# Two unused buffers shift the on-chip addresses of the split weights and of the matmuls' moving operands

## The reference

```python
for l in range(DEPTH):                       # DEPTH = 2
    hp = _modulate(xp, norm1_g[l], ...)      # RMSNorm, shift, scale
    ...                                      # l = 0: differential attention || GQA
    ...                                      # l = 1: mLSTM || latent attention
    xp = xp + mod_p[2] * out_p
    hp = _modulate(xp, norm2_g[l], ...)
    xp = xp + mod_p[5] * _conv_ffn(hp, ffn_w_up[l], ffn_conv_w[l], ffn_conv_b[l], ffn_w_down[l])
    ...                                      # the same for the latent tokens xs
```

## Time and profile before

| | |
|---|---|
| median of three executions | 2651.89 us (2647.7 to 2652.81) |
| the profiled execution | 2675.88 us, of which the span from first to last instruction is 2674.1 us |
| TensorE matmul busy | 2550.9 us, 95% of the span |
| VectorE, ScalarE busy | 1485.3 us, 1295.8 us |
| mean granted clock of TensorE | 0.976 |

### The profile page before, as it was taken

The page is one execution under the profiler, slowest core; times in us unless marked ns, Lnnn a source line. Parts: engine busy times, 40 slices in busy tenths (PEclk is TensorE's granted clock), DMA queues, the critical chain, the costliest instruction groups (busy, mean ns, idle before and its releaser), DMA issues. The chain is left out here.

```text
span 2674.1 us, 52531 instructions
## 1 busy us (share of the span) xinstructions
PE 2550.9 (95%) x20826; PEld 2328.3 (87%) x20826; DVE 1485.3 (56%) x1970; ACT 1295.8 (48%) x1795; POOL 11.7 (0%) x20
## 2 busy tenths in 40 slices
PE   6799999989999999999989999789899999999997
PEld 1487988878888888899989889778899999999997
DVE  1334455655454545577765445645655565567676
ACT  1443444364444444466565444334655555556553
POOL 0000000000000000000000000000000000000000
PEclk9999999989999999999989998889899999999999
DMA  9886665768888888865646884123455555555553
GB/s 388 330 317 233 231 228 184 289 256 309 318 316 319 314 318 313 321 212 192 203 128 234 321 299 142 62 93 114 156 189 186 184 187 185 185 188 187 176 186 107
DMA packets 170060, 608.28 MB, mean 227 GB/s; under 512 B 18688, under 2 KB 25152, under 8 KB 169648
## 3 DMA queue, kind: packets, MB, share of 16 engines
q1 hardware_dynamic: 168624, 600.33, 64.0%
q10 hardware_dynamic: 512, 2.97, 0.3%
q0 software_dynamic: 768, 2.79, 0.3%
HBM read 601.38 MB, written 4.63 MB: 227 GB/s over the span
## 5 line engine op out<-in xcount | busy, mean ns | idle before, releaser
L498 DVE TENSOR_TENSOR w_lo<-raw,w_hi 128x1024 fp32r<-128x1024 f32 x756 | 925.5, 1225 | 966.3 <-ACT w_hi L491 964.6
L491 ACT ACTIVATE w_hi<-raw 128x1024 fp32r<-128x1024 f32 x756 | 798.7, 1057 | 1018.2 <-PE banks L638 994.2
L636 PE MATMUL banks<-xs_ffn,w_hi 128*128 128x256 f32 x4224 | 1188.3, 281 | 5.2 <-DVE xs_ffn L792 5.0
L637 PE MATMUL banks<-xs_ffn,w_hi 128*128 128x256 f32 x4224 | 1181.9, 280 | 0.0
L638 PE MATMUL banks<-xs_ffn,w_lo 128*128 128x256 f32 x4224 | 1181.7, 280 | 0.0
L636 PEld LDWEIGHTS banks<-xs_ffn,w_hi 128*128 128x128 f32 x4224 | 797.8, 189 | 43.5 <-issue 42.6
L638 PEld LDWEIGHTS banks<-xs_ffn,w_lo 128*128 128x128 f32 x4224 | 803.8, 190 | 0.0
L637 PEld LDWEIGHTS banks<-xs_ffn,w_hi 128*128 128x128 f32 x4224 | 795.3, 188 | 0.0
L592 PE MATMUL banks<-raw,cond 128*32 128x512 f32 x1536 | 227.2, 609 | 29.2 <-DMA raw<-in_w_mod 18.0
L636 PE MATMUL banks<-xs_even,w_hi 128*128 128x256 f32 x832 | 241.8, 291 | 10.0 <-DVE w_lo L498 5.9
L637 PE MATMUL banks<-xs_even,w_hi 128*128 128x256 f32 x832 | 233.3, 280 | 0.0
(11 more groups left out here) (305 smaller groups left out, 2054.2 us busy)
## 6 DMA issues: line engine op xcount, KB each, us to landing
raw<-in_w_mod SPq DMA_DIRECT2D x384, 512.0 KB, 6.7
raw<-in_ffn_w_up SPq DMA_DIRECT2D x352, 512.0 KB, 3.5
raw<-in_ffn_w_down SPq DMA_DIRECT2D x176, 512.0 KB, 4.1
raw<-in_even_w_in SPq DMA_DIRECT2D x72, 512.0 KB, 4.0
raw<-in_odd_w_in SPq DMA_DIRECT2D x64, 512.0 KB, 4.5
raw<-in_even_w_out SPq DMA_DIRECT2D x32, 512.0 KB, 3.7
raw<-in_odd_w_out SPq DMA_DIRECT2D x32, 512.0 KB, 3.2
raw<-in_odd_w_tail SPq DMA_DIRECT2D x8, 448.0 KB, 3.7
```

Source lines behind the costliest of these rows:

```text
L491: act.activation(w_hi[:, o % SPLIT], raw[:, s % RAW], ACT.Copy).then_inc(hi_done.sem, 1)
L498: dve.tensor_tensor(w_lo[:, o % SPLIT], raw[:, s % RAW], w_hi[:, o % SPLIT].bitcast(F32), ALU.subtract).then_inc(lo_done.sem, 1)
L636: pe.matmul(made, hi, x_hi, start=start and not second, stop=False, skip_group_check=second)
L637: pe.matmul(made, hi, x_lo, start=False, stop=False, skip_group_check=second)
```

## The change

Two buffers that nothing reads or writes are declared: 96 columns of 4 bytes (384 bytes a partition) between `raw` and `w_hi`, and 16 columns (64 bytes) behind `m0`. By this `w_hi` and `w_lo`, `x` and `const` move by 384 bytes, and all that the stages declare by 448. After it the split weights and the moving operands of all stages begin at multiples of 512 bytes; so before it the split weights began 128 bytes, and the moving operands 64 bytes, behind such a multiple. The tiles inside these buffers step by multiples of 512 bytes. No instruction is added, removed or moved.

```diff
         raw = sb("raw", [P, RAW, CHUNKS, SLABW])
+        weight_pad = sb("weight_pad", [P, 96])
         w_hi = sb("w_hi", [P, SPLIT, CHUNKS, SLABW], F32R)
         w_lo = sb("w_lo", [P, SPLIT, CHUNKS, SLABW], F32R)
...
         m0 = sb("m0", [2 * HEADS, 2])
+        stage_pad = sb("stage_pad", [P, 16])
```

## The result

The changed kernel takes 2739.77 us (2737.51 to 2742.23, six executions), before 2652.06: ratio 1.0319, interval 1.0277 to 1.0362. It is 88 us slower, beyond the forecast range and beyond the price of the rival that named a loss. The kernel before has two times of its own: of 19 executions beside a later experiment twelve took 2646.0 to 2652.2 us and seven 2673.6 to 2678.7; the profiled one is of the second kind. Of the six executions behind this ratio one is (2678.82); the ratio takes the mean of all six.

A forecast was written before the change was run, and what follows sets the result against it. The prediction took TensorE's matmuls, covering 95% of the span, as the bound. Loads, splits and products each counted 0, so the forecast was the unchanged median, 2652 us, with a range of 2630 to 2684 us.

The forecast's parts named there:

- the rival that named a loss: Products from layer 1's feed-forward on: slow pace spreads; 26 us, 2678 us, up to 2707 us; chance 0.26.
- What bounds the kernel: Whole kernel: TensorE's matmuls cover 95% of the span, at two paces, 113.3 and 117.7 ns a product.
- The loads and the splits: Weight and small transfers, and the VectorE and ScalarE splits: cost 0; without cover at most 11 us for splits.
- The term of the products: TensorE's 17,856 products: where operands begin does not set their pace, taken as 0.
- All fast: Bound on the products: every one at the fast pace, together 46 us less.
- all slow: Bound on the products: every one at the slow pace, together 29 us more.
- Rival B: Entry into layer 1's feed-forward turns slow: 26 us, 2678 us; all other places slow too, 2681 or 2707; chance 0.26.
- A: Products everywhere: aligned operands make the slow pace rare, 2606 or 2632 us; chance 0.22.
- C: Products everywhere: alignment removes waste even from the fast pace, 2488 us at the most; chance 0.02.
- The sum: Whole kernel: change of 0 on the profiled 2675.88 us; forecast is the median, 2652 us.

The follow-up runs named there:

- e1: Changed kernel without the second buffer (behind `m0`): split weights at residue 0 of 512, moving operands at 448; 2674.94 us.
- e4: Changed kernel with the first buffer 112 columns instead of 96 and no second buffer: weights at residue 64, moving operands at 0; 2680.52 us.
- e2: Changed kernel without the first buffer (before `w_hi`): split weights and moving operands both at residue 128 of 512; 2736.71 us.
- e3: Changed kernel with the first buffer 112 columns instead of 96: split weights and moving operands both at residue 64 of 512; 2739.18 us.
- f1: Kernel before plus only the second buffer, 32 columns wide: moving operands 64 bytes above the weights (+64); 2681.31 us.
- j1: Kernel before plus 128 unused bytes between `w_hi` and `w_lo` and 384 behind `m0`: moving operands -64 to `w_hi`, +64 to `w_lo`; 2635.60 us, ratio 0.9909.
- i1: Changed kernel without second buffer, 16 unused columns before `w_lo`, feed-forward `x_hi` at residue 0 and `x_lo` at 64 of 256; 2709.84 us.
- i2: Changed kernel without second buffer, 16 unused columns before `w_lo`, feed-forward `x_hi` at residue 64 and `x_lo` at 0 of 256; 2696.15 us.
- j2: Kernel before plus only 128 unused bytes between `w_hi` and `w_lo`: moving operands +64 to `w_hi`, -64 to `w_lo`; median 2668.42 us, ratio 1.0040.

## Why the prediction was wrong

**What bounds the kernel** was right: TensorE's steps set the end, and no other engine's time changed. **The loads and the splits** at 0 were right: the splits still last 1225 and 1056 ns, and the instructions are the same.

**The term of the products, taken as 0, failed.** The change cost 62.5 us between the two traces and 88 us between the medians, and what changed is the step of the products, from 113.3 or 117.8 to 120.0 ns. The prediction said that the operands' begins don't set the pace, on three rows, and each was read for more than it holds.
The first said that two phases with the same addresses go at two paces, so "the address alone cannot decide the pace". True of the choice between these two. But the distance decides which paces there are to choose from: 113.3 and 117.8 ns at 64, 120.0 alone at 0 (e1 and e4 against e2 and e3).
The second took the exchanged roles in `ukv` as another placing. It is +64 against -64, and f1 shows that +64 has the paces of -64. The row could not tell.
The third, 213.3 ns at the lower clock, was to rule out a cost of badly placed operands. The changed kernel, with the cost in every product at full clock, shows the same there (timeline, eleven starts behind the norm's wait):

```profile
557.60 0.41 PE L639 MATMUL banks<-xs_ffn,w_hi 128*128 128x256 f32 x1
...
559.73 0.41 PE L640 MATMUL banks<-xs_ffn,w_lo 128*128 128x256 f32 x1
```

2.13 us for ten steps, 213 ns, at a granted clock of 0.50. At 1.2 GHz the cost does not show, so that row said nothing of 2.4 GHz.

**The bounds failed with it.** "All fast" and "all slow" used the two paces that the trace shows, -46 and +29 us. No row of before has any distance but 64 between these operands, so a slower pace could not be seen, and 117.8 ns was no upper bound for it. Each product is 2.2 ns beyond the bound, 17,856 x 2.2 = 39 us: 29 and 39 make 68, about the 69 worked out above.

**Rival B** had the right side and named the right residue ("both operands beginning at the same residue of 512 could be what tips it"), but put it at one entry, worth 26 us, and at 2707 us with all places at 117.8 ns. It is every product, and at 120.0. **A** and **C** did not happen in the changed kernel; A's state, the slow pace gone, is what j1 has in the feed-forward layers, by another placing than the alignment that A named; C's, a stretch under 113.3 ns, no run had. The 109.2 ns that C took from the Trainium skill (page "TensorE: Matmul & The Clock Gate", section "Back-to-back issue gap") is on that page the figure of a matmul by itself, not of a stream of loads and products, and the three products reached it in no run.

The Trainium skill's rule of 16-byte lines (page "SBUF — State Buffer", section "Specifications (TRN2)") gave 0 too. The same page, section "Who interferes with whom", states that TensorE reads its moving operand and its weights by two independent ports and never waits on anyone. It says nothing of where the two operands lie. Here the step goes from 113.3 to 120.0 ns by the distance between the two alone (e1 and e4 against e2 and e3); the measurement decides.

**The sum** said that timed runs may hold the fast pace in layer 1. That fits: the two groups of times lie about 26 us apart, which is that stretch's price. No timed run left a trace, so it is not shown; and a time alone does not tell which stretch was slow, since f1, at 2681.31 us, has its layer 1 at 113.3 ns and its layer 0 at 117.8.

Open is the mechanism. That the distance of the two operand buffers modulo 256 matters is shown; that TensorE's own accesses meet in the memory is only a guess. Why i1 and i2, and j1 and j2, differ as they do, why some distances have two paces, and what chooses between them, stays open.

## What to carry to other kernels

Where TensorE is the bound, read its step from start to start, not its busy share, and compare it between stages with the same products: 95% busy hid a difference of 4%, and the worst layout 6%. When products and weight loads follow each other without a gap, the distance between the moving buffer and the weight buffer is a parameter to sweep, for each weight buffer of a triple by itself, since beginning both at the same boundary was, with +96, the slowest of all tried. Time each placing more than once: j2's eleven executions of one placing lie 47 us apart. A bound taken from the rows of one layout bounds nothing for another layout.

## What the runs showed of the hardware that was not expected

In these runs a stream of weight load and 256-column product at the 2.4 GHz level steps at 120.0 ns when both operands begin at the same residue of 256 bytes, at 113.3 or 117.8 ns 64 bytes apart, and between 116.6 and 120.0 ns in the stretches at the other distances tried, 32 to 128 bytes, most of them seen in one execution. Where TensorE's stream does not break, a pace once entered is held for hundreds of microseconds (5946 starts in 700 us before, 5836 after). The 120.0 ns hold with VectorE and ScalarE at rest and the DMA engines at a share of 0.01. At the 1.2 GHz level the step is 213 ns with and without the cost. With two weight buffers at -64 and +64 bytes the stretches of both feed-forward layers go at 113.3 ns, with +64 and -64 at 118.9 in the one execution traced. A view that begins 16 bytes off a multiple of 32 was no better than its neighbours (118.4 and 119.2 ns at 48).
